# State-space mixer of a hybrid layer: decay exponents from two 32-row products, squares added on GpSimd, late scaling behind the masked decays

## What is computed

```python
dt = jax.nn.softplus((dt + dt_bias).astype(jnp.float32))
acum = jnp.cumsum((dt * a).reshape(b, n, c, h).transpose(0, 3, 1, 2), axis=-1)
seg = acum[..., :, None] - acum[..., None, :]
decay = jnp.where(causal, jnp.exp(jnp.where(causal, seg, 0.0)), 0.0)
y_diag = jnp.einsum('bgjnqs,bnsgjp->bnqgjp', cb[:, :, None] * decay, xdt)
y_off = jnp.einsum('bnqgd,nbgjpd->bnqgjp', cm, s_prev) * dec_in[..., None]
...
y = (y + xs * d_skip[:, None]).reshape(b, l, SSM_INNER) * jax.nn.silu(z)
y = _rms_norm(y.reshape(b, l, SSM_GROUPS, SSM_INNER // SSM_GROUPS), norm_g, SSM_NORM_EPS)
```

## Time and profile before

| | us |
|---|---|
| median of 3 runs | 1448.69 (1448.61 to 1450.59) |
| span of the profiled execution | 1447.4 |
| TensorE busy in the span | 1422.7 (98%) |
| VectorE, ScalarE, GpSimd busy | 727.2, 411.7, 221.4 |
| the five state-space chunks, 465 to 621 us | 156.3 |

### The profile page before, as it was taken

How to read it: one execution, slowest core, us unless ns; L and a number is a source line. 1 busy time by engine, 2 the same in 40 slices (tenths; PEclk the granted TensorE clock), 3 DMA queues, 4 the chain that set the end, 5 groups by cost and what they waited for, 6 DMA issues and landing times.

```text
span 1447.4 us, 32378 instructions
## 1 busy us (share of the span) xinstructions
PE 1422.7 (98%) x13553; PEld 1031.3 (71%) x13553; DVE 727.2 (50%) x1360; ACT 411.7 (28%) x847; POOL 221.4 (15%) x183
## 2 busy tenths in 40 slices
PE   7999999999999999999999999999999999999997
PEld 6999777677776777777779985864466766757752
DVE  7443778887755677735467654623312112211217
ACT  2333444443422454333533211111111111111112
POOL 3784113130110000020003000011010000000000
PEclk9999999999999999999999999999999999999999
DMA  7897573754244544566568639699999999999996
GB/s 286 190 194 155 129 219 105 205 174 134 73 132 141 140 119 120 185 184 190 150 228 209 213 115 388 244 402 413 425 427 428 428 427 428 428 428 425 430 410 264
DMA packets 157907, 375.76 MB, mean 260 GB/s; under 512 B 102241, under 2 KB 110833, under 8 KB 139841
## 3 DMA queue, kind: packets, MB, share of 16 engines
q1 hardware_dynamic: 141936, 346.64, 67.7%
q0 software_dynamic: 7152, 16.85, 3.4%
q10 hardware_dynamic: 8672, 10.20, 2.1%
HBM read 329.24 MB, written 51.95 MB: 263 GB/s over the span
## 4 chain that ended last, share of the span: by engine, by line
PE 88%; DVE 6%; DMA 2%; DVEq 2%; ACT 1%; issue 1%; SPq 0%; ACTq 0%
PE PS L725 22%; PE PS L1296 15%; PE PS L1315 8%; PE PS L742 7%; PE PS L1142 6%; PE PS L1263 6%; PE PS L809 3%; DVE region L1823 2%; PE PS L1184 2%; PE PS L1268 2%; DVE region L1830 2%; PE PS L1206 1%; DMA region<-w_in 1%; PE PS L817 1%; PE PS L1122 1%
## 5 line engine op out<-in xcount | busy, mean ns | idle before, releaser
L725 PE MATMUL PS<-h0T,region 128*128 128x320 f32 x1360 | 390.3, 438 | 2.9 <-issue 1.6
L1428 ACT ACTIVATE region<-PS 128x320 f32<-128x320 f32 (+5 forms) x351 | 146.0, 427 | 664.8 <-PE PS L725 227.8
L725 PEld LDWEIGHTS PS<-h0T,region 128*128 128x128 f32 x1360 | 251.6, 190 | 110.8 <-issue 12.9
L1296 PE MATMUL PS<-region 128*64 128x512 f32 x1024 | 228.1, 592 | 0.0
L1296 PEld LDWEIGHTS PS<-region 128*64 128x64 f32 x1024 | 117.6, 137 | 101.6 <-issue 49.8
L1823 DVE TENSOR_TENSOR region<-region 128x512 f32<-128x512 f32 (+10 forms) x237 | 165.4, 717 | 35.9 <-DMA region<-wo 5.7
L1428 ACT ACTIVATE region<-region 128x256 f32<-128x256 f32 (+10 forms) x229 | 99.5, 465 | 100.3 <-DVEq L2243 24.5
L1315 PE MATMUL PS<-region,history 128*64 128x512 f32 x512 | 119.2, 597 | 1.1 <-ACTq L1763 0.5
L1823 DVE TENSOR_TENSOR history<-region,PS 128x256 f32<-128x256 f32 x32 | 13.5, 421 | 200.5 <-ACTq L1758 200.5
L1428 ACT ACT_TABLE_LOAD x77 | 98.8, 1283 | 25.5 <-ACTq L1475 9.5
L1830 DVE SCALAR_TENSOR_TENSOR region<-region,feature_vectors 128x320 f32<-128x320 f32 (+1 forms) x103 | 76.9, 747 | 54.1 <-ACTq L1504 41.0
(11 more groups left out here) (248 smaller groups left out, 1582.8 us busy)
## 6 DMA issues: line engine op xcount, KB each, us to landing
region<-moe_w SPq DMA_DIRECT2D x65, 2048.0 KB, 29.8
region<-moe_w SPq DMA_DIRECT2D x65, 1024.0 KB, 28.5
region<-w_in SPq DMA_DIRECT2D x115, 512.0 KB, 5.6
region<-wo SPq DMA_DIRECT2D x32, 512.0 KB, 4.4
expert_rows<-region SPq DMA_DIRECT2D x20, 512.0 KB, 7.0
region<-expert_rows SPq DMA_DIRECT2D x5, 2048.0 KB, 16.6
projected<-region ACTq DMA_DIRECT2D x59, 167.5 KB, 3.6
region<-projected SPq DMA_DIRECT2D x10, 768.0 KB, 6.6
```

Source lines behind the costliest of these rows:

```text
L725: last = mm(PS[:, 6 + i % 2, 0:NTOK], WR[:, i, k, :], H0T[:, k, :], start=(k == 0), stop=(k == KT - 1))
L1296: last = mm(PS[tiles(i), 2, :], XE[:, k, tiles(i)], W13[r][i][:, k * 512:k * 512 + 512], start=(k == 0), stop=(k == KT - 1))
L1428: return nc.scalar.activation(out, in_, f, **kw)
```

## The change

- LH and PM now hold the head rows twice: partitions 32 to 63 serve heads 0 to 15, and a copy on partitions 64 to 95 serves heads 16 to 31. RD shrinks from 16 to 8 blocks of 64 columns, and the two exponent products contract 32 partitions each, at 32 and at 64, into two banks as before. To fill partitions 64 to 95, three small copies are loaded once (near the start of the RWKV phase, counted by `vectors_in`), and the dt rows of a chunk come as two transfers, 64 and 32 partitions (three for chunk 0), so `rows_in` counts 32 a chunk.
- GpSimd adds the four squares of a group in two steps, in place in YO, and signals `squares_summed`; TensorE runs one square-sum product instead of four, behind a `fill(3)` in one piece.
- ScalarE moves `fill(3)` ahead of the root.
- VectorE runs `late(c - 1)` behind the four decay products, not ahead of `step_in`.

```diff
-        LH, PM, SEL, TRI = (... (C_LH, 128), (C_PM, 16), (C_SEL, 32), (C_TRI, 128)))
+        LH, PM, SEL, TRI = (... (C_LH, 128), (C_PM, 8), (C_SEL, 32), (C_TRI, 128)))
...
+            sp.wait_ge(sem("vectors_in"), 32)
+            sp.dma_start(VEC[64:96, V_DTB:V_ALOG + 1], io['vecs'][32:64, V_DTB:V_ALOG + 1]).then_inc(sem("vectors_in"), 16)
+            sp.wait_ge(sem("consts_in_or_rows_kept"), 16)
+            sp.dma_start(CON[64:96, C_LH:C_LH + 128], io['consts'][32:64, C_LH:C_LH + 128]).then_inc(sem("vectors_in"), 16)
+            sp.dma_start(CON[64:96, C_PM:C_PM + 8], io['consts'][32:64, C_PM + 8:C_PM + 16]).then_inc(sem("vectors_in"), 16)
...
-                sp.dma_start(UM, ut[T_MISC, :, c, HIST:CW]).then_inc(sem("rows_in"), 16)
+                sp.dma_start(UM[0:64], ut[T_MISC, 0:64, c, HIST:CW]).then_inc(sem("rows_in"), 16)
+                sp.dma_start(UM[64:96], ut[T_MISC, 32:64, c, HIST:CW]).then_inc(sem("rows_in"), 16)
+                if c == 0:
+                    sp.dma_start(UM[96:128], ut[T_MISC, 96:128, c, HIST:CW]).then_inc(sem("rows_in"), 16)
...
-                    last = mm(bank(3 + k, 8, L), LH, RD[:, 8 * k:8 * k + 8, :], **full)
+                    rows = slice(32 + 32 * k, 64 + 32 * k)
+                    last = mm(bank(3 + k, 8, L), LH[rows], RD[rows], **full)
...
-                fill(3, range(KT // 2))
-                pe.wait_ge(sem("squares"), one)
-                w = bank(5, 4, L, n=256)
-                for k in range(4):
-                    last = mm(w, ONE, YO.rearrange("p (g i) b -> p g i b", i=4)[:, :, k, :], start=(k == 0), stop=(k == 3))
-                last.then_inc(sem("square_sums"), 1)
-                fill(3, range(KT // 2, KT))
+                fill(3)
+                pe.wait_ge(sem("squares_summed"), one)
+                mm(bank(5, 4, L, n=256), ONE, YO.rearrange("p (g i) b -> p g i b", i=4)[:, :, 0, :], **full
+                   ).then_inc(sem("square_sums"), 1)
...
+            pe.wait_ge(sem("vectors_in"), 80)
...
+            act.wait_ge(sem("vectors_in"), 80)
...
+                fill(3)
                 root(RG, "variance", one, "rstd")
-                fill(3)
...
-                dve.wait_ge(sem("rows_in"), c * 16 + 16)
+                dve.wait_ge(sem("rows_in"), c * 32 + 48)
...
-                tt(RD, over(AC, 16, 0, L), PM.unsqueeze(2).to_broadcast([128, 16, L]), mul)
+                tt(RD, over(AC, 8, 0, L), PM.unsqueeze(2).to_broadcast([128, 8, L]), mul)
...
-                if c > 0:
-                    late(c - 1)
                 if c is not NPC:
                     step_in(c + 1)
...
                 dve.drain().then_inc(sem("ss_mt"), 1)
+                if c > 0:
+                    late(c - 1)
                 tt(XET, XDT, ALS.unsqueeze(2).to_broadcast([128, 16, L]), mul)
...
+            dve.wait_ge(sem("vectors_in"), 80)
...
+                pool.wait_ge(sem("squares"), c + 1)
+                sq = YO.rearrange("p (g i) b -> p g i b", i=4)
+                ptt(sq[:, :, 0:2], sq[:, :, 0:2], sq[:, :, 2:4], add)
+                pool.drain()
+                ptt(sq[:, :, 0], sq[:, :, 0], sq[:, :, 1], add)
+                pool.drain().then_inc(sem("squares_summed"), 1)
```

## The result

The changed kernel takes 1455.8 us (median of six runs, 1452.94 to 1458.76) beside 1449.75 us of the kernel before in the same session (1448.61 to 1451.68): a ratio of 1.0041, 95% interval 1.003 to 1.0051, so about 6 us slower. The forecast was no change, 1448.6 with a range up to 1453.5; the time lies above the range.

What follows compares the result with a forecast made beforehand. TensorE bounds the stage before; afterwards a 32.45 us round would pace chunks 1 to 3 (+3.54), TensorE's 29.45 chunks 0 and 4 (-3.64): total -0.10, 1448.6 us, range 1443.5 to 1453.5, chance 0.47.

Steps and rivals of the forecast that it cites:

- TensorE's part: TensorE's own work per state-space chunk falls from 31.27 to 29.45 us: square sums gain 1.31, 32-row exponent products 0.51.
- the round: Chunk-to-chunk chain from square sums through variance, fetch, `step_in` and output back to square sums; 32.45 us, pacing chunks 1 to 3.
- variance to conv issue: Round's step 1, VectorE's variance start to the conv rows' fetch on SyncE: 6.35 us, from 7.31 before.
- `step_in` to output: Round's step 3 on VectorE, with masked decays, late scaling (2.80) and output: 8.72 us including 0.05 for the wake-up.
- output to Square: Round's step 4, from VectorE's output to the start of ScalarE's squares: 5.24 us, as before.
- Square to the end of GpSimd's second add: Round's step 5, squares' start through GpSimd's adds, held by VectorE's state product, to waking TensorE: 4.65 us.
- Step 2: Round's step from the conv rows' fetch issue on SyncE to the dt rows landed: 6.85 us.
- rival A: Rows come sooner, fetch at chunk 0's 5.2 + 0.42; 1444.8 us, or 1443.6 if GpSimd isn't held up; chance 0.22.
- Rival C: Rows come later, in two transfers: 1455.3 us at the worst landing, 1453.2 halfway; decides from fetch 7.9; chance 0.20.
- 1.5 to 2.7 us ahead of the state sums: Sign that the forecast is right: TensorE waits this long there in chunks 1 to 3.
- the 0.9 of waiting that I forecast ahead of the square sums: Sign that the forecast is right: TensorE waits near 0.9 us there in chunks 1 to 3.
- The state load of chunk 4 and the GLA stage keep their distance: Claim that chunk 4's state load and the gated linear attention stage add no cost.

Runs made afterwards that it cites:

- only_late: Kernel before, with only the late scaling moved behind the masked decays; ratio 1.005 to the kernel before.
- store_late: Kernel after, with ScalarE moving the first projection tile and issuing its store behind the decays' exponents; ratio 1.0034 to the kernel before.
- rows_first: Kernel after, with the next chunk's dt rows issued first, ahead of z rows, weights and conv rows; ratio 1.0005 to the kernel before.
- one_piece: Kernel after, with the second piece of the dt rows (rows 64 to 96) left out in chunks 1 to 4; ratio 1.0036 to the kernel before.

## Why the prediction was wrong, step by step

- **TensorE's part** was right. With no wait, a chunk takes 29.41 (29.45 predicted); the square sums alone give 31.27 - 29.96 = 1.31 (1.31), the 32-row products 31.27 - 30.72 = 0.55 (0.51). The four records take 1.13 us, where 0.90 and a mode change of 0.2 were taken. The Trainium skill ("TensorEngine Tiling (Array Packing)", Key Properties) says that a change of tiling mode drains TensorE; the trace agrees, the tile behind these products takes 4.50 on the chain instead of 4.31:

```profile
466.17 1.06 PE PS L999 x4
467.23 4.50 PE PS L733 x16
```

- **That the round takes over** was right, and so were its terms but for the fetch. In chunk 2 of after: variance to conv issue 534.50 - 528.16 = 6.34 (6.35), `step_in` to output 551.19 - 542.53 = 8.66 (8.67), output to Square 556.43 - 551.19 = 5.24 (5.24), Square to the end of GpSimd's second add 560.89 - 556.43 = 4.46, with 0.1 to wake TensorE 4.56 (4.65):

```profile
556.43 1.06 ACT L1435 ACTIVATE region<-region 128x1024 f32<-128x1024 f32 x1 [4.15 <-DVEq L2235]
```
```profile
557.58 2.42 POOL L2831 TENSOR_TENSOR region<-region 128x512 f32<-128x512 f32 x1 [22.26 <-ACTq L1649]
560.15 0.74 POOL L2833 TENSOR_TENSOR region<-region 128x256 f32<-128x256 f32 x1
```

  The first add starts with the Square's end and takes 2.42 instead of 1.27: it is held while VectorE's state product runs, as taken. The Trainium skill ("SBUF — State Buffer", Who interferes with whom) gives this as an exclusive lock; the trace agrees.
- **Step 2, variance's fetch to rows landed, was mis-sized.** 6.85 came from landings of before. In the kernel after it took 7.74 on average (with 0.05 in it), 0.84 more a chunk, 2.5 us in all. The three landings scatter: in only_late, with the queue as before, the fetches were 8.03, 6.48 and 6.67. I had asked what the rows' second piece costs (nothing, as it turned out), and not what else would cross the fetch: the packets of the first tile's store begin 2.9 us behind the conv rows' issue, in the middle of the fetch, where they began 4.4 to 4.6 behind it before (in chunk 0 too, so that store was no argument against rival A), and moving that store away took 0.47 off. Rival C had the sign and the place, with a fetch that decides from 7.9; it came out just under that. That C's 1455.3 lies next to the measured 1455.8 is luck: it needs a fetch of 9.1, and 7.74 alone gives 1451.1. (C's "halfway there, 8.4" isn't halfway from 6.85 to 9.1 either: that is 7.98, and gives 1452.0.)
- **A step was missing: what TensorE's wait does to TensorE.** I had the wait itself ("1.5 to 2.7 us ahead of the state sums"; 2.00 measured) and took TensorE's work behind it at the durations of rows at full clock. Behind the wait the clock fell and the state sums took 3.55 to 3.68 instead of 1.93. Where it did not fall, TensorE is through early and waits 0.69 us for GpSimd's adds (store_late, chunk 3):

```profile
594.95 0.70 PE L1039 MATMUL PS<-region,constants 128*128 128x256 f32 x2 [0.69 <-POOLq L2834]
```

  Where it fell, the path over TensorE became the longer, by 0.7 a chunk. So the 0.9 of waiting that I forecast ahead of the square sums is not there. Three chunks: 2.1 us. The trace of before shows no lower clock until its last 5 us, and no wait of TensorE near 2 us in or behind the stage from which it could have been read; the bounds of my range took none in.
- **"The state load of chunk 4 and the GLA stage keep their distance"**, put at no cost without a row, was wrong: 0.2 us of waiting for the load (in chunk 4 below), and 1.87 us where gated linear attention (GLA) begins. In the total it hardly shows, since before has 1.3 us of waits for weights behind the stage and after 0.45, so the rest of the span grew by 0.4 only.
- **The sum.** -0.10 as predicted, +2.5 for the fetch, +2.1 for the clock, +0.2 for chunk 4 (29.71) makes 4.7 of the 4.8 us by which the stage grew. Neither missed term alone leaves the range; the two together, and a kernel before that took 1.06 us more in these runs than in those of the table (1449.75 against 1448.69), do. The part of the change that the loss hangs on is the late scaling's new place: alone it gives 1.005, and without it the same kernel is at 0.9981. Forecast and rivals all charged it 2.8 us in the round, which was right; both terms that I missed hang on the wait that it opened.

## What to carry to other kernels

Before work that fills the flight of a transfer is moved, find what will be waited for in its place, and move the transfer first (here two lines on SyncE's queue turned 1.0041 into 0.9972, and with the scaling put back into 0.9958). Where a step makes TensorE wait, price the work behind the wait at the lower clock as one bound of the range. When a signal moves behind other work, as the square sum did, follow it into the next stage too. A sum over a round is worth the trouble: it held to 0.01 us once the fetch was measured and where the clock stayed up.

## What the hardware showed unexpectedly

- Idle times of 1.94 to 2.76 us on TensorE in this stage were joined by a fall of the granted clock to 0.50 in 15 of 17 cases over all runs, for 3.41 us (in two of them 6.83), which costs TensorE 1.7 us each (3.0 where it was 6.83, in rows_first). Two waits of 2.01 us (only_late and store_late, chunk 3) had none, and of the ten waits of 1.83 to 2.32 us at the start of gated linear attention only one (one_piece) had it; what tells them apart was not found.
- An issue that stands behind the 3072-packet conv rows on SyncE's queue holds that queue for 2.39 to 4.72 us over all runs, ahead of them for 0.43 to 0.48. A second piece issued behind that did not make the fetch longer.
